# Seven block products for eight in the second feed-forward matrix of both tail blocks

## Reference

```python
def sq_relu_mlp(x, w1, w2):
    return jnp.square(jax.nn.relu(x @ w1)) @ w2      # w1 1024 x 4096, w2 4096 x 1024
...
for i in range(DEPTH):                               # 2
    h = mixer_sb_ssm(...) if i % 2 == 0 else mixer_dsa(...)
    x = layer_norm(ALPHA * x + h, ln_mix_g[i], ln_mix_b[i])
    x = layer_norm(ALPHA * x + sq_relu_mlp(x, mlp_w1[i], mlp_w2[i]), ln_ffn_g[i], ln_ffn_b[i])
```

## Time and profile before

| what | value |
| --- | --- |
| median of 3 runs | 1467.52 us (1467.16 to 1467.55) |
| span of the profiled execution | 1467.4 us |
| PE, DVE, ACT, POOL busy | 98%, 55%, 50%, 20% of the span |
| matmuls | 8640 |
| mean granted clock of PE | 0.997 |
| loaded from HBM | 247.94 MB, 170 GB/s over the span |
| feed-forward part of block A, from its ff1(1) to the end of ff2(7) | about 1000.6 to 1171.2 us |
| the same of block B, to the last instruction | about 1290.4 to 1464.9 us |

### The profile page before, as it was taken

How to read it: one execution, slowest core, us unless ns; L and a number is a source line. 1 busy time by engine, 2 the same in 40 slices (tenths; PEclk the granted TensorE clock), 3 DMA queues, 4 the chain that set the end, 5 groups by cost and what they waited for, 6 DMA issues and landing times.

```text
span 1467.4 us, 19978 instructions
## 1 busy us (share of the span) xinstructions
PE 1442.2 (98%) x8640; PEld 1231.4 (84%) x8640; DVE 814.0 (55%) x1010; ACT 730.8 (50%) x910; POOL 289.6 (20%) x109
## 2 busy tenths in 40 slices
PE   7999999999999999999999999999999999999998
PEld 5788889988877788888989788688998888888986
DVE  5337665454553364854444669875444557554445
ACT  4465635544455554654455366646544336264452
POOL 4598150000029694410000000000000004000000
PEclk9999999999999999999999999999999999999999
DMA  8833345654446543445566353215654453255451
GB/s 302 297 124 128 125 146 198 213 211 180 173 153 236 196 146 116 166 170 210 173 198 219 122 190 115 98 61 183 230 187 172 153 196 115 74 206 209 172 198 60
DMA packets 121222, 250.26 MB, mean 171 GB/s; under 512 B 15040, under 2 KB 27056, under 8 KB 121008
## 3 DMA queue, kind: packets, MB, share of 16 engines
q1 hardware_dynamic: 120872, 248.90, 48.1%
q10 hardware_dynamic: 264, 0.10, 0.0%
HBM read 247.94 MB, written 1.05 MB: 170 GB/s over the span
## 4 chain that ended last, share of the span: by engine, by line
PE 93%; DVE 4%; POOL 1%; issue 1%; ACT 1%; DMA 0%; DVEq 0%
PE psum L464 90%; PE psum L471 4%; DVE x L2572 1%; POOL w_lo L1107 1%; DVE big L2566 1%; DMA work<-in_norm_mix 0%; DVE rows L1379 0%; DVE w_lo L1107 0%; DVE tiny L2615 0%; DVE big L2572 0%; DVE ht_lo L1353 0%; DVE hT L1348 0%; DVE pT L2816 0%; DVE rows L2566 0%; DVE ht_lo L2566 0%
## 5 line engine op out<-in xcount | busy, mean ns | idle before, releaser
L464 PE MATMUL psum<-ht_hi,w_lo 128*128 128x256 f32 x960 | 269.2, 281 | 0.9 <-issue 0.6
L464 PE MATMUL psum<-w_lo,ht_hi 128*128 128x512 f32 (+1 forms) x576 | 222.5, 390 | 0.9 <-DVE w_lo L1107 0.9
L464 PE MATMUL psum<-w_lo,hid_hi 128*128 128x512 f32 x512 | 202.4, 395 | 0.0
L464 PEld LDWEIGHTS psum<-ht_hi,w_lo 128*128 128x128 f32 x960 | 179.7, 187 | 3.2 <-issue 2.0
L1087 ACT ACTIVATE w_hi_work<-ring 128x2048 fp32r<-128x2048 f32 x40 | 76.5, 1913 | 153.2 <-PE psum L464 150.5
L1107 DVE TENSOR_TENSOR w_lo<-ring,w_hi_work 128x2048 fp32r<-128x2048 f32 x29 | 66.5, 2292 | 129.9 <-ACT w_hi_work L1087 129.9
L1177 DVE TENSOR_TENSOR hid_lo<-work,hid_hi 128x512 fp32r<-128x512 f32 x60 | 41.5, 692 | 160.4 <-ACT hid_hi L1155 160.4
L464 PEld LDWEIGHTS psum<-w_lo,ht_hi 128*128 128x128 f32 x576 | 108.5, 189 | 22.5 <-DVE w_lo L1107 1.7
L464 PE MATMUL psum<-ht_lo,w_hi_rows 128*128 128x256 f32 x448 | 125.0, 279 | 0.0
L464 PE MATMUL psum<-ht_lo,w_hi_tmp 128*128 128x256 f32 x448 | 125.0, 279 | 0.0
L464 PE MATMUL psum<-ht_hi,w_hi_tmp 128*128 128x256 f32 x448 | 124.9, 279 | 0.0
(11 more groups left out here) (399 smaller groups left out, 3382.9 us busy)
## 6 DMA issues: line engine op xcount, KB each, us to landing
ring<-in_w_ff SPq DMA_DIRECT2D x32, 2048.0 KB, 7.9
ring<-in_mlp_w SPq DMA_DIRECT2D x32, 2048.0 KB, 8.4
ring<-in_w_in SPq DMA_DIRECT2D x19, 2048.0 KB, 8.1
ring<-in_w_out SPq DMA_DIRECT2D x4, 2048.0 KB, 8.1
ring<-in_w_ple_gate SPq DMA_DIRECT2D x4, 2048.0 KB, 8.0
ring<-in_sb_ssm_w_in SPq DMA_DIRECT2D x4, 2048.0 KB, 8.9
ring<-in_dsa_w_in SPq DMA_DIRECT2D x3, 2048.0 KB, 8.7
ring<-in_w_up_nsa SPq DMA_DIRECT2D x2, 2048.0 KB, 8.4
```

The source lines that it names most:

```text
L464: ins = pe.matmul(o, lhsT, rhs, start=start, stop=stop)
```

## The change

The matrix product of ff2.n (hidden values of 512 units by 256 tokens, with 512 by 1024 weights) is seen as a two by two block product: token halves A1, A2 with the hidden units in halves (A11, A12, A21, A22), and weights B11, B12, B21, B22. For n = 0 to 6 in both blocks it is made with seven block products in place of eight, each of two matmul groups of 512 columns, from sums of blocks:

- DVE makes four sums of weight blocks (`dve_form_sums`, 1024 columns each), ACT copies six forms to high digits (one of 2048 columns, five of 1024), DVE makes the six low ones (`dve_form_lows`). Of the hidden values DVE makes four sums of 256 columns, ACT their high and DVE their low digits (1024 columns).
- The seven products are summed over n in banks 1 to 7. Bank 0 alone is left for the hidden units of ff1.2 to ff1.7; these tiles are therefore split by columns, and PE does unit 0, the first eight matmuls of the block product (`seven_first`), unit 1, and the other 34 (`seven_rest`). The low digits of ff1.2 to ff1.7 are now made on POOL (`lower_columns`).
- After n = 6 DVE adds the banks up into x (`dve_seven_products`, ten instructions of 512 columns); ff2(7) is multiplied as before, into banks 4 to 7, where the fourth waits until bank 7 is read.

```diff
+POOL_SPLITS += [f"{pre}ff1.{n}" for pre in SEVEN for n in range(2, LAST + 1)]
...
+            def ff1_unit(n, q, w):
+
+                lo, hi = w
+                wait_split(f"{pre}ff1.{n}", q)
+                _, nth = wide_.next(f"{pre}f{2 * n + q}")
+                pe.wait_ge(wide_.saved.sem, st.at(wide_.saved, nth + 1))
...
+                    for k in range(KT):
+                        last = k == KT - 1
+                        products(bank[0][:, u * S:(u + 1) * S], hi(k, c), lo[:, k, c], ht_hi[:, k, :], ht_lo[:, k, :],
+                                 k == 0, last, wide_.ready if last and u == 1 else None)
...
+            def seven_first(n, lo):
...
+                pe.wait_ge(form_hi.sem, st.at(form_hi, 6 * m + 1))
+                pe.wait_ge(hid_lo_ready.sem, st.at(hid_lo_ready, FB // 2 * mlp_nth(pre) + 2 * n + 2))
+                if n == 0:
+                    pe.wait_ge(wide_.saved.sem, st.at(wide_.saved, wide_.nth_save(f"{pre}f3")))
+                for o, v in ((bank[4], 1), (bank[1], 0)):
+                    for u in range(2):
+                        f = s + 2 * u + v
+                        mm(o, hid_lo[:, f, 0:P], col_hi[:, u, v, :], n == 0 and u == 0, False)
+                        mm(o, hid_hi[:, f, 0:P], col_hi[:, u, v, :], False, False)
...
+            def seven_rest(n, lo):
...
+                pe.wait_ge(form_lo.sem, st.at(form_lo, 6 * m + 1))
+                for o, v in ((bank[4], 1), (bank[1], 0)):
+                    for u in range(2):
+                        mm(o, hid_hi[:, s + 2 * u + v, 0:P], w[:, u, v, 0:BANK], False, n == LAST - 1 and u == 1 and v == 0)
+                sh, sl = s_hi[n % 2], s_lo[n % 2]
+                pe.wait_ge(s_low.sem, st.at(s_low, m + 1))
+                rest = [(bank[5], 3, b22_hi, w[:, :, 1, BANK:D]), (bank[7], 0, t1_hi, w[:, :, 0, BANK:D]),
+                        (bank[3], 2, t_hi[0], t_lo[0]), (bank[2], 1, t_hi[1], t_lo[1])]
+                for i, (o, form, hi, low) in enumerate(rest):
+                    pe.wait_ge(form_lo.sem, st.at(form_lo, 6 * m + 2 + i))
+                    for u in range(2):
+                        products(o, s_form(sh, form, u), s_form(sl, form, u), hi[:, u, :], low[:, u, :], n == 0 and u == 0,
+                                 n == LAST - 1 and u == 1 and i > 0, None)
+                pe.wait_ge(form_lo.sem, st.at(form_lo, 6 * m + 6))
+                for u in range(2):
+                    f = s + 2 * u + 1
+                    products(bank[6], hid_hi[:, f, P:S], hid_lo[:, f, P:S], t_hi[2][:, u, :], t_lo[2][:, u, :],
+                             n == 0 and u == 0, False, seven_done if n == LAST - 1 and u == 1 else None)
+
...
+                    if pre in SEVEN and q == 3:
+                        pe.wait_ge(seven_read.sem, st.at(seven_read, mlp_nth(pre) + 1))
...
+                        first = k == 0 and (q == 3 if pre in SEVEN else n == 0)
...
+            if pre in SEVEN:
+                ff1(1)
+                lo = seven_open(0)
+                seven_first(0, lo)
+                seven_rest(0, lo)
+                tile_done()
+                for n in range(2, LAST + 1):
+                    w = next_columns(f"{pre}ff1.{n}")
+                    ff1_unit(n, 0, w)
+                    lo = seven_open(n - 1)
+                    seven_first(n - 1, lo)
+                    ff1_unit(n, 1, w)
+                    tile_done()
+                    seven_rest(n - 1, lo)
+                    tile_done()
...
+    def lower_columns(st, pool, tiles, splits, name):
...
+        for h in range(2):
+            c = slice(h * S, (h + 1) * S)
+            pool.wait_ge(w_hi_ready.sem, st.at(w_hi_ready, 2 * nth + h + 1))
+            pool.tensor_tensor(w_lo[n % RING][:, :].rearrange("p (k n) -> p k n", k=KT)[:, :, c],
+                               ring[n % RING][:, :].rearrange("p (k n) -> p k n", k=KT)[:, :, c],
+                               w_hi[PLACES2[name][h]][:, :].rearrange("p (k n) -> p k n", k=KT).bitcast(F32), ALU.subtract) \
+                .then_inc(st.up(w_lo_pool), 1)
...
+    def forms_free(st, eng, tiles, pre, n):
+
+        before = f"{pre}ff2.{n - 1}" if n else {"A.": "sbo1", "B.": "dso1"}[pre]
+        eng.wait_ge(tile_used.sem, st.at(tile_used, tiles.index(before) + 1 + RING))
...
+        act.activation(col_hi, w[:, :, :, 0:BANK], ACT.Copy).then_inc(st.up(form_hi), 1)
+        act.activation(b22_hi, w[:, :, 1, BANK:D], ACT.Copy).then_inc(st.up(form_hi), 1)
...
+        act_hidden_forms(st, act, pre, 0)
+        hidden(2)
+        act_sum_forms(st, act, tiles, pre, 0, (2, 3))
+        hidden(3)
+        act_split(st, act, tiles, splits, f"{pre}ff1.2")
+        act_hidden_forms(st, act, pre, 1)
+        for n in range(2, LAST + 1):
+            ahead = f"{pre}ff1.{n + 1}" if n < LAST else f"{pre}ff2.{LAST}"
+            act_plain_forms(st, act, tiles, pre, n - 1)
+            act_sum_forms(st, act, tiles, pre, n - 1, (0, 1))
+            hidden(2 * n)
+            act_sum_forms(st, act, tiles, pre, n - 1, (2, 3))
+            act_split(st, act, tiles, splits, ahead, (0,))
+            hidden(2 * n + 1)
+            act_split(st, act, tiles, splits, ahead, (1,))
+            if n < LAST:
+                act_hidden_forms(st, act, pre, n)
...
+        b11, b12, b21, b22 = (w[:, :, v, c * BANK:(c + 1) * BANK] for v in range(2) for c in range(2))
+        dve.wait_ge(tile_in[at % RING].sem, st.at(tile_in[at % RING], 16 * (at // RING + 1)))
+        forms_free(st, dve, tiles, pre, n)
+        for o, a, b in ((t_sum[0], b22, b12), (b12, b12, b11), (t_sum[1], b22, b12), (t_sum[2], b21, t_sum[1])):
+            dve.tensor_tensor(o, a, b, ALU.subtract).then_inc(st.up(t_summed), 1)
+            dve.wait_ge(st.last.sem, st.reached())
...
+        forms = ((1, lo[:, :, :, 0:BANK], w[:, :, :, 0:BANK], col_hi), (2, lo[:, :, 1, BANK:D], w[:, :, 1, BANK:D], b22_hi),
+                 (4, lo[:, :, 0, BANK:D], w[:, :, 0, BANK:D], t1_hi), (3, t_lo[0], t_sum[0], t_hi[0]),
+                 (5, t_lo[1], t_sum[1], t_hi[1]), (6, t_lo[2], t_sum[2], t_hi[2]))
+        for i in which:
+            nth, low, v, hi = forms[i]
+            dve.wait_ge(form_hi.sem, st.at(form_hi, 6 * m + nth))
+            dve.tensor_tensor(low, v, hi.bitcast(F32), ALU.subtract).then_inc(st.up(form_lo), 1)
+
...
+    def dve_hidden_sums(st, dve, pre, n):
+
+        h = hid_f[:, 4 * (n % 2):4 * (n % 2) + 4, :].rearrange("p (u v) t -> p u v t", v=2)
+        a11, a12, a21, a22 = (h[:, :, v, t * P:(t + 1) * P] for t in range(TT) for v in range(2))
+        s1, s2, s3, s4 = (s_form(s_sum[n % 2], i) for i in range(4))
+        dve.wait_ge(hid_hi_ready.sem, st.at(hid_hi_ready, FB // 2 * mlp_nth(pre) + 2 * n + 2))
+        dve.tensor_tensor(s1, a21, a22, ALU.add).then_inc(st.up(dve_step), 1)
+        dve.tensor_tensor(s3, a11, a21, ALU.subtract).then_inc(st.up(dve_step), 1)
+        dve.wait_ge(st.last.sem, st.reached())
+        dve.tensor_tensor(s2, s1, a11, ALU.subtract).then_inc(st.up(dve_step), 1)
+        dve.wait_ge(st.last.sem, st.reached())
+        dve.tensor_tensor(s4, a12, s2, ALU.subtract).then_inc(st.up(s_summed), 1)
+        dve.wait_ge(st.last.sem, st.reached())
...
+        dve_hidden_sums(st, dve, pre, 0)
+        for f in range(2):
+            dve_hidden_low(st, dve, pre, f)
+        dve_form_lows(st, dve, tiles, pre, 0, (0, 1, 2, 3))
+        dve_hidden_sums_low(st, dve, pre, 0)
+        dve_form_lows(st, dve, tiles, pre, 0, (4, 5))
+        for n in range(1, LAST):
+            dve_hidden_sums(st, dve, pre, n)
+            for f in (2 * n, 2 * n + 1):
+                dve_hidden_low(st, dve, pre, f)
+            dve_hidden_sums_low(st, dve, pre, n)
+            dve_form_sums(st, dve, tiles, pre, n)
+            dve_form_lows(st, dve, tiles, pre, n, range(6))
+        lower_half(st, dve, tiles, splits, f"{pre}ff2.{LAST}", 0)
+        for f in (2 * LAST, 2 * LAST + 1):
+            dve_hidden_low(st, dve, pre, f)
+        lower_half(st, dve, tiles, splits, f"{pre}ff2.{LAST}", 1)
...
+        dve.wait_ge(seven_done.sem, st.at(seven_done, mlp_nth(pre) + 1))
+        scaled(half[0][1], bank[7])
+        scaled(half[1][1], bank[7])
+        scaled(half[0][0], bank[1])
+        scaled(half[1][0], bank[3])
+        dve.tensor_copy(y_sum, bank[1]).then_inc(st.up(dve_step), 1)
+        dve.wait_ge(st.last.sem, st.reached())
+        added(y_sum, y_sum, bank[2])
+        dve.wait_ge(st.last.sem, st.reached())
+        added(half[0][1], half[0][1], y_sum)
+        added(half[1][0], half[1][0], y_sum)
+        added(y_sum, y_sum, bank[3])
+        dve.wait_ge(st.last.sem, st.reached())
+        added(half[1][1], half[1][1], y_sum, seven_read)
...
-            stt(xv, xv, ALPHA, scores[:, n * BANK:(n + 1) * BANK], ALU.mult, ALU.add).then_inc(st.up(ff2_saved), 1)
+            tt(xv, xv, scores[:, n * BANK:(n + 1) * BANK], ALU.add).then_inc(st.up(ff2_saved), 1)
...
+        for n in range(2, LAST + 1):
```

(57 more changed lines are left out.)

79 lines of the change are left out of this document (76 added, 3 removed).

## The result

The changed kernel takes 1525.65 us (median of 4 runs, 1523.42 to 1526.39) against 1467.53 us before (4 runs, 1467.16 to 1467.89): ratio 1.039, 95% interval 1.0376 to 1.0405. It is 58.1 us slower. The prediction was 1525.5 us. The profiled execution took 1526.39 us with a span of 1524.6 us.

What follows compares the result with a forecast made beforehand. DVE's two-input work plus POOL's holds, which exclude each other, were to bound the periods in place of PE. Per block 6.1 + 19.9 + 0.5 + 2.5 = 29.0 us, twice 58.0 on 1467.4: forecast 1525.5 us, 8 in 10 range 1502 to 1547.

Steps and rivals of the forecast that it cites:

- What binds: In the periods: DVE's operations with two SBUF inputs and POOL's exclude each other, so DVE sets the pace; chance 0.77.
- Six periods of 25.8: Per block, n = 1 to 6: each period takes 25.8 us against 22.48, +19.9 us a block.
- its 16.9: DVE's own work per period in us: 17.6 less about ten starts 0.09 earlier, without POOL's holds.
- The column form: Rival: POOL's subtraction by columns costs 5.9 us in the periods, +31 us, 1556 us in all; chance 0.05.
- Side by side (1463.5 to 1466.9): Rival: DVE and POOL run without excluding each other in the periods; of 1463.5 to 1466.9 us the lower; chance 0.06.
- Head: Start of each block: PE waits 4.8 us ahead of `seven_first`(0), plus 1 and 1.7, less 1.4 saved: +6.1 us.
- The slow clock: Start of a block: PE's clock falls after its wait ahead of `seven_first`(0) and loses 1.7 us, estimated.
- DVE's first lows and POOL's first operation: Start of a block, behind PE's wait: these cost about 1 us, estimated.
- Slow clock in the periods: Rival: PE's clock falls in every period, 1.7 us in each of 12, +20 us, 1546 us; chance 0.03.
- End of the block: ff2(7)'s second low half some 0.5 us late, then DVE's final chain 2.5 us later, per block.
- Sum: Both blocks: 6.1 + 19.9 + 0.5 + 2.5 = 29.0 us each, twice 58.0, giving 1525.5 us.
- PE's spare time of 4.7 us a period: In the periods: PE has 4.7 us to spare, so losses from its slow clock are mostly absorbed.

Runs made afterwards that it cites:

- e1: Changed kernel, but DVE instead of POOL makes the low digits of ff1.2 to ff1.7 in both blocks: 1467.13 us.
- e2: Changed kernel, but POOL only fills unused SBUF in place of its subtractions; PE reads high digits of ff1.2 to ff1.7 for the low ones: 1466.35 us.
- e8: Changed kernel, but POOL's two operations per tile are copies with one SBUF input in place of subtractions with two: 1466.18 us.
- e5: e1 together with e3's order at the start of each block, where ACT saves hidden units 2 and 3 before the hidden forms: 1466.84 us.
- e3: Changed kernel, but at each block's start ACT saves hidden units 2 and 3 first and DVE makes the hidden sums' low digits second: 1521.16 us.
- e4: Changed kernel with six more matmuls of 512 columns per tile given back to PE in `seven_rest`: 1536.56 us.

## Why the prediction was right, by its steps

- **What binds.** Right. The exclusion between POOL's reading operations and DVE's with two SBUF inputs makes the loss: e1 takes it away, e2 does so with POOL still busy, e8 makes it short enough for PE to hide, and all end within 1.7 us of the kernel before. The Trainium skill says in "SBUF — State Buffer", section Who interferes with whom, that a VectorE instruction with two SBUF inputs contends with a GpSimd instruction that reads SBUF and not with one that only writes it. The traces agree: in e2 DVE stays at 1.22 beside fills of 2.04 us, in e8 it is longer by 1.7 beside copies.
- **Six periods of 25.8.** Measured 25.83, so +20.1 per block for the predicted 19.9. Both parts of the sum can be seen alone: DVE is busy 16.90 us in e2's window, and POOL's 24 operations in the two blocks of the changed kernel hold the way for 4.39 to 4.49 us each, counted from the end of the DVE operation that was running (the first of each block is the exception told below); 16.90 + 2 x 4.47 = 25.84. Two small things cancel in this: DVE's list has some 0.2 us of gaps between operations that wait for each other (in e5 it is 21.38 long and 21.14 busy), and a DVE operation beside one of POOL's is longer by 4.3 to 4.4 us and not by 4.47. The prediction reached its 16.9 by a slip, too: ten starts 0.09 earlier take 17.6 to 16.7, which would have made the forecast 2.4 us lower. That the slip hit the right value was luck. The column form costs POOL nothing extra: the operations at 1044.75 and 1028.13 take 4.9 and 4.8 us with the wait ahead of them in it, so that rival is out.
- **Side by side (1463.5 to 1466.9).** Its condition wasn't met. Its price was right: e2, where the two engines do run side by side, took 1466.35 us, near the upper end and not the lower one that the prediction took. The saved matmuls are real (in e1 the period drops by 1.36 us, 22.49 to 21.13) and are taken up by head and finish even without POOL.
- **Head.** Predicted 4.8 us of waiting and 6.1 in all; measured 4.88 and 17.58 - 11.03 = 6.55. Two of its terms were off and nearly cancel. The slow clock was put at 1.7 us and cost 2.9 (42 matmuls in 12.70 us for 9.80). DVE's first lows and POOL's first operation were put at 1 us and cost PE nothing there. From start to start of the matmuls the wait is 5.0 us longer than a step without one, and 5.0 + 2.9 - 1.4 = 6.5. Nor is the head a term that can be undone alone: e3 cut the wait to 1.04 and block A took as long.
- **Slow clock in the periods.** Behind the 3.8 us waits PE's clock fell too (mean 0.51 in the window 1056 to 1062). The periods came out as DVE's and POOL's sum all the same, so DVE's chain covers it; the rival of 1546 us is out.
- **End of the block.** The term was too large: 0.5 + 2.5 predicted. Measured, ff2(7) starts 0.3 late (idle time, on issue), and the aggregation comes 1519.02 - 1504.30 = 14.7 us behind it for token half 1 in block B against 1461.77 - 1448.74 = 13.0 before: 1.7, and the same for token half 0. DVE's ten operations take 6.4 us for the predicted 6.8 and begin 0.2 ahead of ff2(7), where the prediction had them 0.25 behind; the two adds after them find their banks ready.
- **Sum.** 6.55 + 20.08 + 0.32 + 1.66 = 28.61 for block A; with B's 28.32 and the 0.32 ahead of A it is 57.25, against 57.2 between the spans (1524.6 - 1467.4). The prediction had 29.0 and 58.0. It had 0.4 too little in the head, 0.2 too little in the periods and 1.0 too much at the end, and these partly cancel. The agreement at the median within 0.2 us is luck: the runs of the changed kernel alone spread by 3 us.
- **Wrong in the picture.** A wait of 4 us in each period was forecast; there are 3.8 + 1.4 + 1.5 in every second one. And PE's spare time of 4.7 us a period is not free to use: e4 hid on average 0.55 of each added 1.4 us ((9.8 - 5.94) / 7), and the wait that grew is that of DVE's sums for the tile that PE holds longer.

## What to carry to other kernels

Before a subtraction is put on an idle GpSimd, add its whole duration to VectorE's (DVE's) work of that period, as long as that work has two SBUF inputs, and compare the sum with the period of the engine that binds; a shorter or write-only operation may be free where a 4.5 us one costs nearly its full length (e8, e2). If VectorE has the room, doing it there costs half (2.28 us in e1). And a scheme that saves matmuls in the loop pays at both ends of the block: in e1 six periods save 1.36 us each, 8.2 a block, and the head (17.25 - 11.03 = 6.2), the 0.3 and the finish (1.7) take 8.2, so even without contention nothing is left.

## What the runs showed of the hardware

- Who gets in first isn't fixed. POOL's operation at 1021.18 took 6.99 us: three DVE operations started after it and went first (the second of 1020.68, 1022.95, 1023.29), and it got its way only at about 1023.7, where DVE's list has an operation that waits for the one before. The one at 1044.75 got in at the next boundary of DVE after 0.4 us, between operations that also follow each other closely, and so did 21 others of the 24. The other exception is the first one of block B (1340.14, 7.00 us), and e8's first copy of each block waited in the same place; in e3, with another order of DVE's list, the first one (1019.52) got in at once. What decides it stays open.

```profile
1020.68 2.36 DVE L1335 TENSOR_TENSOR t_lo<-big,t_hi 128x1024 fp32r<-128x1024 f32 x2
...
1021.18 6.99 POOL L1249 TENSOR_TENSOR w_lo<-ring,w_hi_tmp 128x2048 fp32r<-128x2048 f32 x1 [163.97 <-ACT w_hi_tmp L1211]
...
1022.95 0.42 DVE L1343 TENSOR_TENSOR work<-work 128x256 f32<-128x256 f32 x1
1023.29 0.42 DVE L1344 TENSOR_TENSOR work<-work 128x256 f32<-128x256 f32 x1
1023.75 4.71 DVE L1346 TENSOR_TENSOR work<-work 128x256 f32<-128x256 f32 x1
```

- POOL copies 2048 columns in about 1.9 us (e8, at 1046.26, with no DVE operation ahead of it) where its subtraction of that size holds the way for 4.47.
